# One inference step of a two-layer decoder on one core: the cached keys of a sequence multiplied as one pair of pages, a sequence behind their transposes

## The reference

```python
# prompt tokens: an indexer scores the keys, the best 64 are kept, attention over them
valid = (idx <= tpos[None, :, None])[:, :, None, :]
p = jax.nn.softmax(jnp.where(valid, s, NEG), axis=-1)          # s = q . k * ATTN_SCALE
# sample tokens: keys and values come from the paged cache and from the new tokens
phys = jax.vmap(lambda pt, pi: pt[pi])(page_table, page_idx)
k_sel = cache_k[phys, off]
v_sel = cache_v[phys, off]
s_pool = jnp.einsum('bthd,btkhd->bthk', q, k_sel).astype(jnp.float32)
s = jnp.where(is_new, s_new, s_pool) * ATTN_SCALE
p = jax.nn.softmax(jnp.where(valid, s, NEG), axis=-1)          # 65 kept of 260
o = jnp.einsum('bthk,btkhd->bthd', p_pool, v_sel) + jnp.einsum('bthj,bjhd->bthd', p_new, v)
```

## Time and profile before

| | |
|---|---|
| median of 3 runs | 1523.28 us (1520.26 to 1525.46) |
| span of the profiled execution | 1521.1 us, 2.2 us below the median; a time of its own beside the span isn't given for it |
| PE busy | 1506.2 us, 99% of the span |
| DVE, ACT, POOL busy | 1211.3, 992.1, 165.2 us |
| attention loop on PE | 148.05 to 191.49 us |
| behind it, to the first value product | 191.49 to 196.94 us |
| pair stage | 196.94 to 216.60 us |

### The profile page before, as it was taken

The page is one execution under the profiler, slowest core; times in us unless marked ns, Lnnn a source line. Parts: engine busy times, 40 slices in busy tenths (PEclk is TensorE's granted clock), DMA queues, the critical chain, the costliest instruction groups (busy, mean ns, idle before and its releaser), DMA issues.

```text
span 1521.1 us, 21932 instructions
## 1 busy us (share of the span) xinstructions
PE 1506.2 (99%) x8350; PEld 1285.5 (85%) x8350; DVE 1211.3 (80%) x1106; ACT 992.1 (65%) x955; POOL 165.2 (11%) x162
## 2 busy tenths in 40 slices
PE   9999999999999999999999999999999999999998
PEld 7887779999997987888888888888888888888887
DVE  3589687666455768888888889888889888888887
ACT  3444565444345567777777777777778777777775
POOL 2555000000000035501001001000000000100100
PEclk8999999999999999999999999999999999999999
DMA  7651873525646349999999999999999999999990
GB/s 215 233 224 57 332 285 111 194 84 197 219 168 211 111 136 374 354 394 384 394 393 384 394 393 383 395 393 382 396 393 378 386 384 361 381 395 376 373 367 32
DMA packets 198857, 456.94 MB, mean 300 GB/s; under 512 B 12021, under 2 KB 15135, under 8 KB 198795
## 3 DMA queue, kind: packets, MB, share of 16 engines
q1 hardware_dynamic: 190802, 439.34, 78.0%
q0 software_dynamic: 4336, 13.15, 3.0%
q10 hardware_dynamic: 3656, 3.60, 0.8%
HBM read 444.04 MB, written 12.03 MB: 300 GB/s over the span
## 4 chain that ended last, share of the span: by engine, by line
PE 85%; DVE 2%; ACT 1%; issue 0%; DVEq 0%; ACTq 0%
PE bank L2057 19%; PE bank L2569 13%; PE bank L2571 13%; PE bank L2570 13%; PE bank L2583 7%; PE bank L2585 7%; PE bank L2584 7%; PE bank L2593 2%; PE bank L2340 1%; PE bank L2344 0%; DVE wql L1842 0%; PE bank L2544 0%; PE bank L2537 0%; PE bank L2044 0%; PE bank L2081 0%
## 5 line engine op out<-in xcount | busy, mean ns | idle before, releaser
L1842 DVE TENSOR_TENSOR wql<-ring,wqh 128x2048 fp32r<-128x2048 f32 x335 | 766.7, 2291 | 107.7 <-ACT wqh L994 106.9
L994 ACT ACTIVATE wqh<-ring 128x2048 fp32r<-128x2048 f32 x334 | 641.3, 1920 | 230.5 <-PE bank L2571 148.1
L2569 PE MATMUL bank<-wqh,xgh 128*128 128x512 f32 x892 | 353.6, 396 | 0.3 <-DVE wql L1842 0.3
L2570 PE MATMUL bank<-wql,xgh 128*128 128x512 f32 x896 | 349.1, 390 | 0.0
L2571 PE MATMUL bank<-wqh,xgl 128*128 128x512 f32 x892 | 348.0, 390 | 0.0
L2571 PEld LDWEIGHTS bank<-wqh,xgl 128*128 128x128 f32 x892 | 167.4, 188 | 35.9
L2569 PEld LDWEIGHTS bank<-wqh,xgh 128*128 128x128 f32 x892 | 167.5, 188 | 34.3 <-DVE wql L1842 1.1
L2570 PEld LDWEIGHTS bank<-wql,xgh 128*128 128x128 f32 x896 | 168.5, 188 | 32.8
L994 ACT ACTIVATE wd<-ring 128x1024 fp32r<-128x1024 f32 x90 | 95.1, 1059 | 133.5 <-PE bank L2057 133.5
L2583 PE MATMUL bank<-wqh,heTh 128*128 128x512 f32 x440 | 171.4, 389 | 0.0
L2585 PE MATMUL bank<-wqh,heTl 128*128 128x512 f32 x440 | 171.2, 389 | 0.0
(11 more groups left out here) (453 smaller groups left out, 2065.6 us busy)
## 6 DMA issues: line engine op xcount, KB each, us to landing
ring<-in_moe_w_gate SPq DMA_DIRECT2D x56, 2048.0 KB, 14.0
ring<-in_moe_w_up SPq DMA_DIRECT2D x56, 2048.0 KB, 14.1
ring<-in_moe_w_down SPq DMA_DIRECT2D x56, 2048.0 KB, 13.7
ring<-in_attn_w_in SPq DMA_DIRECT2D x7, 2048.0 KB, 13.1
ring<-in_ffn_w_gate SPq DMA_DIRECT2D x5, 2048.0 KB, 10.3
ring<-in_ffn_w_up SPq DMA_DIRECT2D x5, 2048.0 KB, 7.9
ring<-in_cache_k SPq DMA_DIRECT2D x16, 512.0 KB, 7.0
ring<-in_cache_v SPq DMA_DIRECT2D x16, 512.0 KB, 5.6
```

The lines of the kernel that those rows point to most:

```text
L994: return nc.scalar.activation(dst, src, ACT.Copy)
L1842: return v.tensor_tensor(dst, src, head.bitcast(F32), ALU.subtract)
L2569: mm(bank, xgh[:, k, :], w_h[:, part], start=(k == 0), stop=False)
L2570: mm(bank, xgh[:, k, :], w_l[:, part], start=False, stop=False)
```

## The change

Two pages of a sequence are now multiplied together. `keys_dot(b)` makes per head one product of 256 columns, eight sets instead of sixteen. The transposed keys lie in `keys_of(b)`: `KT` for even sequences, the first 2048 columns of `hE` for odd ones. The set of sequence `b - 1` stands at the end of step `b`, behind both transposes of sequence `b`; `take_kt` waits for the set two sequences back.

The loop's order changes with it. The scores of a unit come first, then `keys_turn(2b)`, the turned probabilities of the unit before, `keys_turn(2b + 1)`, the sum of unit `b - 2`, and the set. The last turned probabilities and the last two sums stand behind the loop, and the mask product `mrep` moves from step 7 to step 6. VectorE copies both of its key banks ahead of `softmax_out`. The 12 spare products behind the loop become 5.

In the pair stage, the `own` copies move from ahead of the `stat` copies to behind `value_head(3)`, with a semaphore `own_ok` of their own. The last page of a pair finishes the first half's bank before it starts the second. `heads_of_pair` waits for ScalarE's half before head 0, and for VectorE's only before head 4.

```diff
     for b in range(NSEQ):
-        if b == NSEQ - 1:
+        if b == NU:
             A.add("mrep", "dve")
         if b < NU:
             A.add(("s", b), "dve")
+        A.add(("ktr", 2 * b, 0), "act")
+        A.add(("ktr", 2 * b, 1), "dve")
+        if 1 <= b < NU:
+            A.add(("pt", b - 1), "act")
         A.add(("ktr", 2 * b + 1, 0), "act")
         A.add(("ktr", 2 * b + 1, 1), "dve")
...
+    def keys_of(b):
+        place = KT[:].rearrange("p a h s -> p (a h s)") if b % 2 == 0 else \
+            hE[:].rearrange("p k t -> p (k t)")[:, 0:PAGES * H * P]
+        return place.rearrange("p (h g s) -> p h g s", h=H, g=PAGES)
...
         def take_kt(n):
             act.wait_ge(*A.full(("ktr", n, 0)))
-            if n >= 2:
-                act.wait_ge(kt_free, n - 1)
-            copy(KT[:, n % 2, 0:4, :], A.ap(("ktr", n, 0))[:].rearrange("p (h s) -> p h s", h=4)).then_inc(a_act, 1)
+            if n >= 2 * PAGES:
+                act.wait_ge(kt_free, n // 2 - 1)
+            copy(keys_of(n // 2)[:, 0:4, n % 2, :], A.ap(("ktr", n, 0))[:].rearrange("p (h s) -> p h s", h=4)).then_inc(a_act, 1)
...
         for g in range(2):
             bank = A.ap(("spt", g))
             act.wait_ge(*A.full(("spt", g)))
-            copy(own[:, P * g:P * g + P], bank[0:NS, 2 * P:3 * P])
...
         for n in range(3, NPG):
             value_head(n)
+            if n == 3:
+                for g in range(2):
+                    act.wait_ge(*A.freed(("spt", g)))
+                    last = copy(own[:, P * g:P * g + P], A.ap(("spt", g))[0:NS, 2 * P:3 * P])
+                last.then_inc(own_ok, 1)
...
+            take_kt(2 * b)
             take_kt(2 * b + 1)
             if b < NU:
                 softmax_out(b, P, nh, w, half)
-            if 2 * b + 2 < NPG:
-                take_kt(2 * b + 2)
...
             for h in range(H):
                 g, rows, q0 = h // 4, slice(NS * (h % 4), NS * (h % 4) + NS), NS * (NSEQ * h + b) - TS * b
-                last = mm(B.ap(("ss", g))[rows, P * pg:P * pg + P],
-                          qz[:].rearrange("p n c -> p (n c)")[:, q0:q0 + NS], KT[:, n % 2, h, :],
-                          start=False, stop=(n == NPG - 1), skip_group_check=True)
...
+                last = mm(B.ap(("ss", g))[rows, 0:PAST],
+                          qz[:].rearrange("p n c -> p (n c)")[:, q0:q0 + NS],
+                          keys_of(b)[:, h, :, :].rearrange("p g s -> p (g s)"),
+                          start=False, stop=(b == NSEQ - 1), skip_group_check=True)
...
-        spare(A.ap(("spt", 0)), value_heads(1)[:, 0:P], value_heads(1)[:, 0:CH], 12)
+        spare(A.ap(("spt", 0)), value_heads(1)[:, 0:P], value_heads(1)[:, 0:CH], 5)
...
+                final = n == 4 * i + 3
+                steps = [(half, low) for half in range(2) for low in range(2)] if final else \
+                    [(half, low) for low in range(2) for half in range(2)]
...
-            pe.wait_ge(*A.freed(("ov", i, 0)))
-            pe.wait_ge(*A.freed(("ov", i, 1)))
             final = i == NSEQ // 2 - 1
             for h in range(H):
+                if h % 4 == 0:
+                    pe.wait_ge(*A.freed(("ov", i, h // 4)))
```

More of the change, by code:

```diff
@@ L425, in build @@
             A.add(("s", b), "dve")
+        A.add(("ktr", 2 * b, 0), "act")
+        A.add(("ktr", 2 * b, 1), "dve")
+        if 1 <= b < NU:
+            A.add(("pt", b - 1), "act")
         A.add(("ktr", 2 * b + 1, 0), "act")
         A.add(("ktr", 2 * b + 1, 1), "dve")
-        if 1 <= b <= NU:
-            A.add(("pt", b - 1), "act")
-        if 2 * b + 2 < NPG:
-            A.add(("ktr", 2 * b + 2, 0), "act")
-            A.add(("ktr", 2 * b + 2, 1), "dve")
-        if 2 <= b <= NU + 1:
+        if 2 <= b < NU:
             A.add(("o", b - 2), "act")
+    A.add(("pt", NU - 1), "act")
+    for u in range(NU - 2, NU):
+        A.add(("o", u), "act")
     for g in range(2):
@@ L2291, in _ @@
                 last.then_inc(a_full, 1)
+            keys_turn(2 * b)
+            if 1 <= b < NU:
+                turn_probabilities(b - 1)
             keys_turn(2 * b + 1)
[L2293 to L2314 removed]
+            if 2 <= b < NU:
+                values_of_unit(b - 2)
+            if b:
+                keys_dot(b - 1)
+        turn_probabilities(NU - 1)
+        keys_dot(NSEQ - 1)
+        for u in range(NU - 2, NU):
+            values_of_unit(u)
         A.room(pe, ("spt", 0))
         pe.wait_ge(v_head, 2)
[L2317 removed]
+        spare(A.ap(("spt", 0)), value_heads(1)[:, 0:P], value_heads(1)[:, 0:CH], 5)
         for g in range(2):
@@ L2337, in values_of_pair @@
                 left = stat[:, n % 2, n // 2, :]
-                for half in range(2):
+                final = n == 4 * i + 3
+                steps = [(half, low) for half in range(2) for low in range(2)] if final else \
+                    [(half, low) for low in range(2) for half in range(2)]
+                for half, low in steps:
                     part = slice(CH * half, CH * half + CH)
-                    read = mm(outs[half], left, value_heads(n)[:, part], start=(n == 4 * i), stop=False)
-                read.then_inc(v_used, 1)
-                for half in range(2):
-                    part = slice(CH * half, CH * half + CH)
-                    last = mm(outs[half], left, value_page(n, ring_r)[:, part], start=False, stop=(n == 4 * i + 3))
-                    if n == 4 * i + 3:
+                    page = value_page(n, ring_r) if low else value_heads(n)
+                    last = mm(outs[half], left, page[:, part], start=(n == 4 * i and not low), stop=(final and low == 1))
+                    if half and not low:
+                        last.then_inc(v_used, 1)
+                    if final and low:
                         last.then_inc(a_full, 1)
         def heads_of_pair(i):
-            pe.wait_ge(*A.freed(("ov", i, 0)))
-            pe.wait_ge(*A.freed(("ov", i, 1)))
             final = i == NSEQ // 2 - 1
             for h in range(H):
+                if h % 4 == 0:
+                    pe.wait_ge(*A.freed(("ov", i, h // 4)))
                 rows, c0 = slice(NS * (h % 4), NS * (h % 4) + NS), SEL0 + NS * h - 2 * TS * i
```

110 lines of the change are left out of this document (52 added, 58 removed).

## The result

The changed kernel takes 1513.5 us (median of 7 runs, 1510.78 to 1515.72) beside 1520.26 us for the kernel before (median of 7 runs in the same session, 1517.28 to 1525.46). The ratio is 0.9941, with a 95% interval of 0.9921 to 0.9961; the two medians divide to 0.9956. So the change makes it faster by 0.4 to 0.6%. One run of the kernel before, beside e13 to e16, took 1655.63 us at a mean granted clock of 0.848 and is in none of the ratios. The span of the profiled execution went from 1521.1 to 1509.1 us.

The account below looks back on a forecast made before the run. TensorE, busy 99% of the span, was taken as the bound. Terms 1.2 + 3.1 - 1.1 + 1.55 + 0.35 - 0.2 + 0.3 = 5.2 us took the median from 1523.3 to 1518.1 us, range 1514.5 to 1523.

Parts of the forecast that it names:

- hidden anyway: Rival, experts: weight transfers set the pace, so TensorE's lead ends in waits; gain 0 to 1 us, 1522.8 us; chance 0.09.
- The wide sets: Attention loop: eight sets of 256 columns at 1.0 us replace sixteen at 0.575 us, gaining 1.2 us (1.8 to 0).
- The wide sets overlap badly: Rival, loop: a set's second four products wait for the first four; 1.32 us a set, 1520.7 us; chance 0.09.
- the estimate of 1.25 us: Loop: a wide set's time by the skill page's packing rule; the sets would then lose 0.8 us, giving about 1520.
- The waits that go and come: Loop: TensorE's 3.1 us of waits on key copies go; new waits, mainly for first turned probabilities, cost 1.1 us.
- The waits come back: Rival, loop: turned probabilities are late every step, 3 us of waits replacing the old ones; 1521.1 us; chance 0.17.
- Spares: Behind the loop: seven fewer spare products, with a small wait for the sample softmax, gain 1.55 us (1.67 to 0).
- copies: Ahead of the first value product: own and stat copies and idle time leave the chain, gaining 0.35 us.
- The last pair: End of pair stage: half the final set's products go before VectorE's half is ready, gaining 0.3 us (0 to 0.5).
- The slip of 0.2 us: Pair stage: own copies behind ScalarE's fourth value page hold up VectorE's tails, costing 0.2 us (0 to 0.5).
- The slower rival: Rival, loop's end: the clock drops to 1.2 GHz over 9.4 us of work, giving 1527.5 us; chance 0.05.
- The base: Whole kernel: the profiled span lies 2.2 us under the median shown, 1523.3 us, from which the gain is taken.

Follow-up runs that it names:

- e13: Changed kernel with VectorE's first value tail moved from step 1 to step 3 and turned probabilities of units 0 and 1 one page later: 1513.01 us, ratio 0.9949.
- e16: Changed kernel unaltered, timed a third time beside the kernel before: 1510.93 us, ratio 0.9934.
- e1: Changed kernel with each set of 256 columns split into two sets of 128 columns, side by side at the same place: 1515.1 us (1 run).
- e2: Changed kernel with sets of 128 columns standing apart, the first behind the first page's transposes, the second at the step's end: 1513.07 us (1 run).
- e14: Changed kernel with only VectorE's first value tail moved from step 1 to step 3: 1513.54 us (1 run).
- e3: Changed kernel with 12 spare products instead of 5 behind the loop: 1512.6 us (1 run).
- e4: Changed kernel with own copies back ahead of stat copies, a pair's last page in old order, and final sets waiting for both halves: 1515.63 us (1 run).
- e6: Changed kernel with 20 instead of 15 warm-up products ahead of TensorE's first work: 1512.19 us, ratio 0.9938.
- e8: Changed kernel with ScalarE's first value page moved from ahead of unit 0's exponentials to behind unit 1's: 1512.83 us, ratio 0.995.
- e7: Kernel before with 20 instead of 15 warm-up products: 1520.94 us, ratio 0.9997.
- e9: Changed kernel with the turned probabilities of units 0 and 1 one page later, behind their step's second page: 1511.41 us, ratio 0.9929.
- e12: Kernel before unaltered, profiled a second time: 1523.74 us.
- e15: Changed kernel with late turned probabilities, VectorE's first value tail in step 3 and 26 warm-up products: 1511.62 us, ratio 0.9944.
- e5: Changed kernel unaltered, timed again beside the kernel before: 1513.52 us, ratio 0.9949.

## Why the prediction was wrong, point by point

**What bounds the kernel.** Right. The chain lies on TensorE for 93%, and what it gained in the attention reached the end: in the two sessions that timed the changed kernel again the lowest times are 6.5 and 6.8 us apart, where the profiles' stages have 6.60. The rival "hidden anyway" falls.

**The wide sets.** The price of 1.0 us was right (1.00). The term was still mis-sized, and it is the first of two steps that failed: "This part gives 9.2 - 8.0 = **1.2 us**". I charged the old sets with their own starts only. Next to a set the transposes also took 0.97 instead of 0.88 us and the turned probabilities behind it 0.49 instead of 0.43. A step lost 0.30 us (5.43 to 5.13) where I had 0.15; over eight sequences that is 2.4 us instead of 1.2. e1 and e2 settle that it is the number of separate sets that costs, not the width. "The wide sets overlap badly" falls with the 1.00. The extra 128 columns of a set took 1.00 - 0.575 = 0.43 us, what one product of 256 columns over the whole array takes in the scores (0.87 for two). For this shape the estimate of 1.25 us falls too, which came from the rule of the Trainium skill, "TensorE: Matmul & The Clock Gate", Part 3: the measurement decides.

**The waits that go and come.** The 3.1 us went, and more than they. The prediction counted the waits that the profile lists, three of them. In four more places of the first three steps a set came late without a line of its own: the transposes ahead of it take 1.05 to 1.08 us from start to start, where 0.97 is usual. TensorE's timeline of the kernel before, one of the four:

```profile
154.06 1.04 PE L2250 MATMUL bank<-ident,ring 128*128 128x128 f32 x8
155.12 0.64 PE L2264 MATMUL bank<-KT,qz 128*32 128x128 f32 x16
```

And VectorE's copy of the page that this set reads:

```profile
154.29 0.68 DVE L1639 COPY KT<-bank 128x512 f32<-128x512 f32 x1
```

The copy ends at 154.97 and the set starts 0.15 us later; in all four places the set starts 0.15 us behind the end of such a copy. These four come to 0.4 us, and the three listed places take another 0.2 beyond what is listed. So 3.7 us of waiting on key copies went. The new waits were forecast as 1.1 and came to 1.6: 1.12 listed at the first turned probabilities (forecast 0.9), 0.2 beyond it in the blocks on its two sides, about 0.3 hidden in step 2's block lengths (forecast 0.2), and none in steps 3 to 5. The mechanism, the row of work that opens the loop on VectorE, was right, as e13 and e14 show by taking it apart, but for the part that ScalarE holds. "The waits come back" falls.

The loop so sums to 3.7 + 2.4 - 1.6 = 4.5 us, and 4.48 were measured, where the forecast was 3.2. The largest part of the gap is the sets' neighbours (1.2), then the waits that no line lists.

**Spares, copies, the pair stage.** The spares gave 1.47 against 1.55, confirmed by e3. The way to the value product 0.34 against 0.35, but that is partly luck: e4 gives the `own` copies only 0.18 of it, and e3 gives 0.15 to the spares. The last pair 0.30 against 0.3. The slip of 0.2 us for the copies that come back behind the fourth value page did not occur: the pair stage is shorter by just the 0.30 that e4 gives back, and its last value product starts 17.17 us behind its first, where that was 17.16 before.

**The clock.** The slower rival had the clock fall in the loop's end. That did not happen in any of the 15 profiles with the new order; that order's loop repeats to 0.01 us.

**The base.** The second step that failed: "It lies 2.2 us under the median shown, so the median goes from 1523.3 to **1518.1 us**". The three runs of that median are among the seven of the result, whose median is 1520.26; the four others have 1518.9. With 1520.3 as its base, the forecast's own 5.2 us give 1515.1; with 1523.3 and the measured 6.6 it is 1516.7. Either error alone stays in the range, both together give 1513.7, and 1513.5 was measured. That the kernel before came out at 1520.26 here was in part chance: in a later session its median was 1523.55 again. The fault is that a range whose lower end was 3.6 us under the forecast left so little room for it. The warning stood in the earlier trace rows: a stretch at 0.68 in the start says that this execution lost time that others may not lose. I used that row for a rival and not for the base, nor for the width of the range.

## What to carry to other kernels

Price a small block by the step with and without it, from the rows on both sides of it: its neighbours carried half of its cost here. Where run-to-run spread is as large as the forecast gain, compare the lowest times or those at full granted clock too, and look whether the profiled execution itself lost clock ahead of the place that is changed. Count waits from block to block, and not only those that are listed: 0.6 of 3.7 us here had no line. When a wait is removed at the opening of a pipeline, follow the in-order engine until its row has caught up; moving one consumer alone moves the wait.

## What the runs showed of the hardware

The granted clock fell in the same two places in either kernel, in some executions and not in others. At the start, TensorE waits for the indexer's parameters behind its warm-up: in 11 of 18 profiles for 0.9 us or more, and in 6 of these (the first of before, e4, e6, e8, e13, e14) the clock fell within the next microseconds; in the 7 others, with shorter waits or none, it did not. The wait is not enough by itself: e16 waited 1.5 us at full clock. A start with the fall reached the first products with 32 columns at 145.6 to 147.8 us, one without at 143.1 to 144.3. The second place is the router's end and the experts' start near 550 us: 7 of 18 profiles fell (the first of before, e7, e1, e9, e12, e15, e16), e12 the most, with a span of 1522.1 us in spite of its full start; 26 warm-up products do nothing for that.

Within a kernel the times follow the mean granted clock: before took 1517.3 us at 1.000, 1520 at 0.997 and 1525.1 at 0.994; after 1510.8 at 1.000 and 1515.2 at 0.996. Why one execution falls and the next does not stays open. The profiles are too few to tell whether either kernel is more prone to it (1 of 3 of the old order fell at the start, 5 of 15 of the new), but the timed runs point to the old one. Of the 58 runs of the kernel before that were timed beside e5 to e16 (the one of 1655.63 us left out) 6 had a mean granted clock of 0.999 or more, and the mean of all was 0.9965. Of the 24 of the changed kernel unaltered, 9 had it, and their mean was 0.9978. That fits medians that lie further apart than the stages' 6.60 us. Which part of the change would do that is not shown.

Sixteen transposes in a row (1.9 us), and steps of which 2.2 of 5.13 us are transposes, ran at a granted clock of 1.00 throughout.
